# Moving the operand region of a two-block transformer kernel by 64 bytes

## The reference, cut to what matters

```python
def reference(x, ...):
    x = first_block(x, ...)          # 256 rows of 2048 float32, one layer
    return second_block(x, c, ...)   # two layers

# first block: rmsnorm; proj = u @ w_in; a gated delta net and a block attention (8 heads each)
mix = sigmoid(gate_a) * (y_a @ w_branch_gdn) + sigmoid(gate_b) * (y_b @ w_branch_moba)
h = x + mix @ w_out
u = rmsnorm(h)
h = h + (silu(u @ w_ffn_gate) * (u @ w_ffn_up)) @ w_ffn_down

# second block: mod = silu(c) @ w_mod + b_mod, then two attention layers, each
h = x * (1 + scale) + shift
y = attention(h @ w_in) @ w_out      # differential attention, then forgetting attention
x = layer_norm(alpha * x + gate * y)
```

## The kernel before, in words

| tile | start | start modulo 256 | holds |
|---|---|---|---|
| raw, w_hi, w_lo | 16512, 32896, 49280 | 128 | the weight ring |
| xs | 65664 | 128 | the residual, 2 x 2048 columns |
| keep | 82048 | 128 | constants, the identity among them |
| stage | 87488 | 192 | what comes out of PSUM |
| gemv_w | 95680 | 192 | weights of the modulation |
| the region | 105792 | 64 | u, s, hid, mix, ya, yb, ws_hi, ws_lo, gates, lng_bc, lnb_bc, gate_bc, gate_bias, q_d and all other tiles of the stages |

## Time and profile before

### The profile page before, as it was taken

How to read it: one execution, slowest core, us unless ns; L and a number is a source line. 1 busy time by engine, 2 the same in 40 slices (tenths; PEclk the granted TensorE clock), 3 DMA queues, 4 the chain that set the end, 5 groups by cost and what they waited for, 6 DMA issues and landing times.

```text
span 2540.2 us, 38236 instructions
## 1 busy us (share of the span) xinstructions
PE 2498.4 (98%) x14496; PEld 2131.2 (84%) x14496; DVE 1802.6 (71%) x2341; ACT 1156.0 (46%) x1476; POOL 0.2 (0%) x4
## 2 busy tenths in 40 slices
PE   8999999999999999999999999999999989999998
PEld 8987878788888888888888888899988778999886
DVE  6897677676667777777776777777787665656666
ACT  4544333365544544444443334344486344444642
POOL 0000000000000000000000000000000000000000
PEclk9999999999999999999999999999999999999999
DMA  7777676786768888888887777889845545676464
GB/s 216 239 253 255 209 256 217 256 275 212 259 223 277 275 281 280 280 284 278 282 280 254 260 258 257 288 286 296 265 141 193 188 160 176 206 242 181 134 222 142
DMA packets 317516, 605.72 MB, mean 238 GB/s; under 512 B 27310, under 2 KB 31412, under 8 KB 315708
## 3 DMA queue, kind: packets, MB, share of 16 engines
q1 hardware_dynamic: 301628, 571.59, 69.5%
q10 hardware_dynamic: 15744, 32.15, 3.6%
HBM read 593.03 MB, written 10.62 MB: 238 GB/s over the span
## 4 chain that ended last, share of the span: by engine, by line
PE 90%; DVE 4%; DMA 2%; ACT 2%; issue 1%; ACTq 0%; SPq 0%; DVEq 0%
PE bank L666 22%; PE bank L668 22%; PE bank L667 22%; PE bank L691 5%; PE bank L693 5%; PE bank L692 5%; PE bank L609 2%; DMA gemv_w<-in_w_mod 1%; PE bank L796 1%; DVE w_lo L1942 1%; DVE gemv_acc L1961 1%; DVE conv_out L2090 1%; ACT w_hi L1291 1%; DMA gates<-spill 1%; PE bank L1129 1%
## 5 line engine op out<-in xcount | busy, mean ns | idle before, releaser
L1942 DVE TENSOR_TENSOR w_lo<-raw,w_hi 128x1024 fp32r<-128x1024 f32 x820 | 1001.7, 1224 | 649.8 <-ACT w_hi L1291 647.7
L1291 ACT CAST w_hi<-raw 128x1024 fp32r<-128x1024 f32 x820 | 861.3, 1052 | 1289.8 <-PE bank L668 960.7
L666 PE MATMUL bank<-w_hi,u_hi 128*128 128x512 f32 x1216 | 486.0, 400 | 0.5 <-DVE w_lo L1942 0.5
L668 PE MATMUL bank<-w_hi,u_lo 128*128 128x512 f32 x1216 | 477.7, 393 | 0.0
L667 PE MATMUL bank<-w_lo,u_hi 128*128 128x512 f32 x1216 | 474.9, 391 | 0.0
L1961 DVE SCALAR_TENSOR_TENSOR gemv_acc<-gemv_w,small,gemv_acc 128x512 f32<-128x512 f32 x480 | 358.6, 747 | 40.4 <-DMA gemv_w<-in_w_mod 23.3
L666 PE MATMUL bank<-w_hi,s_hi 128*128 128x512 f32 x744 | 298.4, 401 | 1.6 <-DVE w_lo L1942 1.5
L668 PE MATMUL bank<-w_hi,s_lo 128*128 128x512 f32 x744 | 292.8, 394 | 0.0
L667 PE MATMUL bank<-w_lo,s_hi 128*128 128x512 f32 x744 | 291.2, 391 | 0.0
L691 PE MATMUL bank<-s_hi,w_hi 128*128 128x256 f32 x1024 | 283.0, 276 | 0.0
L692 PE MATMUL bank<-s_lo,w_hi 128*128 128x256 f32 x1024 | 282.9, 276 | 0.0
(11 more groups left out here) (365 smaller groups left out, 2870.1 us busy)
## 6 DMA issues: line engine op xcount, KB each, us to landing
gemv_w<-in_w_mod SPq DMA_DIRECT2D x384, 256.0 KB, 3.2
raw<-in_w_in SPq DMA_DIRECT2D x176, 512.0 KB, 4.5
raw<-in_a_w_in SPq DMA_DIRECT2D x128, 512.0 KB, 5.0
raw<-in_w_ffn_gate SPq DMA_DIRECT2D x88, 512.0 KB, 4.6
raw<-in_w_ffn_up SPq DMA_DIRECT2D x88, 512.0 KB, 4.3
raw<-in_w_ffn_down SPq DMA_DIRECT2D x88, 512.0 KB, 4.3
gemv_w<-in_kv_w_mod SPq DMA_DIRECT2D x128, 256.0 KB, 4.0
raw<-in_kv_w SPq DMA_DIRECT2D x64, 512.0 KB, 3.8
```

What stands on the lines that cost most here:

```text
L666: pe.matmul(o, xh, w_hi[:, s, t], start=(k == 0), stop=False)
L668: ins = pe.matmul(o, xl, w_hi[:, s, t], start=False, stop=(k == 2 * units - 1))
L1291: act.copy(w_hi[:, s], raw[:, s]).then_inc(hi_done, 1)
L1942: dve.tensor_tensor(w_lo[:, s], raw[:, s], w_hi[:, s].bitcast(F32), ALU.subtract).then_inc(lo_done, 1)
```

## The change

The region begins 64 bytes later. Every tile in it moves by 64 bytes; nothing outside it moves. The region's start modulo 256 becomes 128, that of the weight tiles; stage and gemv_w stay at 192. The last tile ends at 229248.

```diff
 MOD_FIRST, MOD_REST = 22, 10
+OPERANDS_AT = 64
...
-        region = at[0]
+        region = at[0] + OPERANDS_AT
         K8 = 8 * 1024
```

## The result

The changed kernel takes 2551.68 us (median of 7, 2550.17 to 2554.2), the kernel before, run again beside it, 2544.18 us (7 runs, 2541.82 to 2545.99): a ratio of 1.0031, 95% interval 1.0019 to 1.0042. It is slower by some 7.5 us, where no change was forecast.

The account below looks back on a forecast made before the run. TensorE's matmul count times the distance between starts bounds the kernel; all four terms were 0 on a 2540.2 us span, plus 1.8 and 0.4, giving 2542.4 us. The range 2508 to 2577 us held 0.80.

Parts of the forecast that it names:

- What bounds the kernel: TensorE, 98% busy and 90% of the chain: time is the matmul count times the distance between starts.
- How much hangs on it: 7776 matmuls of 512 columns and 4224 of 256: one nanosecond each is 7.8 us and 4.2 us.
- Steps 1 and 2: VectorE, ScalarE and the transfers: each costed at 0 us.
- Step 3: Transposes at line 609: 273 ns at 0 or 64 bytes apart, read as 0 ns per matmul.
- Step 4: Products at 512 and 256 columns: addresses taken not to set their extra 15.5 and 6.6 ns, so 0 ns.
- first argument: 256-column products show 113.3 and 117.5 ns at the same 64 bytes apart, so the level changes without an address change.
- second argument: From 1650 to 1825 us, matmuls average 113.5 ns beside busy VectorE and ScalarE: traffic at other addresses does not reach TensorE.
- third argument: Counter-evidence: thin products (lines 767 to 769), already 0 apart, are slowest of their size, 120.0 ns; order and PSUM place differ.
- Rival (a): Lines 691 to 693: aligned operands collide, 256-column matmuls at 120 ns, +22.8 us, 2565.2 us; chance 0.20 including smaller losses.
- Rival (c): Aligned operands suit TensorE's two reads: 4.4 ns off every 512-column matmul, 34 us, 2508 us, floor 2393; chance 0.22.
- smaller loss: Any slowdown up to 2577 us, without a place of its own; shares the 0.20 chance of Rival (a).
- Rival (b): 512-column products also slow, to 233 ns: 35 us alone, 2577 us, or 2600 us with Rival (a); chance 0.08.

Follow-up runs that it names:

- both_moved_64: Whole of SBUF, weight ring and region alike, begins 64 bytes later (16576 for 16512) than in the kernel before; 2543.81 us against 2544.0, ratio 1.0001.
- the second experiment: Kernel before with only ws_hi and ws_lo of the first thin product 64 bytes later; 2543.97 us in a single run.
- the last experiment: Kernel before with only u2, hid and mix (and mod_rows behind them) 64 bytes later; 2536.31 us against 2544.31, ratio 0.9966.

## Why the prediction was wrong

**What bounds the kernel** held. TensorE's distance between starts carries the difference: +10.4 us for the two kinds of product, against 10.0 between the spans.

**How much hangs on it** held: 7.8 us per nanosecond on the 512-column matmuls, 4.2 on the others. The change gave -2.2 ns on most of the first (228.9 to 226.7) and +6.7 or +2.2 on the second (113.3 or 117.8 to 120.0). The prediction's 117.5 was read from 12 matmuls; over whole triples this level is 353.3 ns, 117.8 each.

**Steps 1 and 2** held: the pair on VectorE took 2284 and 2282 ns, and the waits on transfers are no part of the difference.

**Step 3** was true of the transposes (273 ns before and after) and worthless for the products. The weakness that it named was the point: plain fp32 matmuls, 128 columns at a time, show nothing at 0 or 64 bytes apart, the fp32r products do. A row of another type is no bound for a row of this one.

**Step 4 is the step that failed.** It put the products at 0 ns; they measured -11.3 us on the 512-column ones and +21.7 us on the 256-column ones. Its first argument was that the 256-column products show 113.3 and 117.5 ns with the same relation of addresses, so that addresses do not set the level. The relation goes with which levels occur, and something else selects among them: at d = -64 there are two for 256 columns, 340 and 353 ns, in 999 and 386 triples, and both_moved_64, with the same relation, has 1114 and 272. At d = 0 none of the 1408 is at 340 and 11 are under 357. In the traces the switch from one to the other comes only where the stream of these products was interrupted, or within three triples behind such a place. Such a place is a wait, a few small matmuls in between, the start of a product, or a short stretch in which the granted clock was lower: 0.52, the 1.2 GHz level, from 114.9 to 117.9 us in the kernel before, behind a wait of 2.3 us, which the 40 slices of the earlier trace rows are too coarse to show. The order of the work does not fix the level either: behind that stretch 53 triples in a row are at 353 ns in the kernel before and 53 at 340 in both_moved_64. What in an interruption decides is not shown. Here are 39 matmuls of that stretch, first before, in 4.60 us (117.9 ns), then both_moved_64, in 4.42 us (113.3 ns):

```profile
120.28 0.28 PE L691 MATMUL bank<-u_hi,w_hi 128*128 128x256 f32 x1
...
124.88 0.28 PE L691 MATMUL bank<-u_hi,w_hi 128*128 128x256 f32 x1
...
120.05 0.28 PE L691 MATMUL bank<-u_hi,w_hi 128*128 128x256 f32 x1
...
124.47 0.28 PE L691 MATMUL bank<-u_hi,w_hi 128*128 128x256 f32 x1
```

That a quantity varies under fixed X does not show that X has no part in it. Its second argument, that VectorE's and ScalarE's traffic leaves TensorE's step alone, was borne out (1542 matmuls at 113.5 ns beside a busy VectorE), and it spoke on the wrong pair: what matters here is the relation of TensorE's own two operands, the moving one and the one that the weight load reads. The third argument was the one to weigh. The thin products were the only rows of the same type and size with the new relation, twice, at 120.0 ns, and the two differences that I held against them turned out to have no part that shows (the second experiment). Rows nearest to the question were outvoted by rows that were more numerous.

The rule cited from the Trainium skill, "SBUF — State Buffer", section "SBUF: two separate sides", that TensorE never waits on anyone for SBUF, speaks of one engine waiting for another. Nothing here contradicts it in that sense, but it could not carry a 0 for the products, because it leaves out how TensorE's own two operands stand to each other: d alone moves the distance between 226.7 and 234.3 ns.

**The rivals.** Rival (a) put the 256-column products at 120 ns, +22.8 us, with some 1460 matmuls in the window from 1650 to 1825 us; measured were 119.9 and 120.0 ns, +21.7 us and 1461. Its mistake was to leave the 512-column products untouched. Rival (c), a gain there, came true at the same time, with 2.2 ns in place of the 4.4 that I had taken from the steps between levels: -11.3 us in place of -34. I had set them up as alternatives, and gave the time of either, not of both, so the measured 2551.7 us falls under the "smaller loss" that I had added to (a) without a mechanism. One relation of addresses acts on both kinds, so their prices had to be summed. Rival (b), 233 ns, is what d = +64 gives, not d = 0.

**The size.** Against the median of before as forecast, 2542.4, the change came out at 2551.7, 9.3 us more; some 1.8 us of that is the kernel before itself, whose median over more runs is 2544.2.

## What to carry to other kernels

When TensorE is the bound with fp32r operands, read the distance between matmul starts to the nanosecond, product by product, and try the relative start of moving and stationary tile modulo 256 as a parameter of its own for each kind of product: it was worth from -0.3% to +2.2% of this kernel with not one instruction changed. Any edit that grows or drops a small tile ahead of others shifts that relation for all that follow, so a regression after such an edit may come from there. No run here tried another kernel or another type. Where one edit acts on two kinds of work, sum the prices; and take the nearest row of the same type over any number of rows of another.

## What the runs showed of the hardware

- In this kernel the distance between back-to-back fp32r matmuls with a weight load each depends on the start of the region tile minus that of the weight tile, modulo 256: from 226.7 ns (d = 0) to 234.3 ns (d = +96) for 512 moving columns, from 113.3 ns (d = -64) to 120.0 ns (d = 0 and +96) for 256. The best value for 512 columns, d = 0, is together with +96 the worst for 256. The two levels at +96, from its timeline, 90 matmuls to each pair:

```profile
1413.99 0.39 PE L667 MATMUL bank<-w_hi,hid_hi 128*128 128x512 f32 x1
...
1435.08 0.40 PE L667 MATMUL bank<-w_hi,hid_hi 128*128 128x512 f32 x1
...
1680.39 0.28 PE L692 MATMUL bank<-s_hi,w_hi 128*128 128x256 f32 x1
...
1691.17 0.29 PE L692 MATMUL bank<-s_hi,w_hi 128*128 128x256 f32 x1
```

- At d = 0 both kinds cost 32 cycles of 2.4 GHz over their columns (226.7 and 120.0 ns against 213.3 and 106.7).
- A triple can hide unequal distances: for hid at d = -64 the next start follows 231.4 ns after the first matmul, 226.0 after the second and 229.4 after the third; at d = -96 it is 232.0, 231.6 and 236.4, and at +64 they are equal, 233.3 or 233.4.
- At d = -64, and once at -192, there are two lasting levels at the same addresses (340 and 353 ns for 256 columns; at -64 also 687 and, in 28 triples with s, 700 ns for 512). The 256-column ones change only at or just behind an interruption of the products; what decides is open.
- fp32 transposes (273 ns) and VectorE with two SBUF operands (2285 and 2282 ns) show none of this at 0 and 64 bytes apart.

What stays open: why. The runs show that the two operands' relation sets the level, not what in the memory or in TensorE makes it so, nor why the eight values come out as they do. That the pattern repeats after 256 bytes rests on one pair of values. Steps under 32 bytes have no measurement. Moving only u and s, the complement of the last experiment, was not tried, because tiles that are in use at the same time lie directly behind them.
